# Three projections of a block by seven products, with the vector sums that they need, and a silu moved ahead

## The chip, the cores and the metric

The kernel runs on one core of one Trainium2 chip. The time is the device time of an execution in microseconds (us); the kernel before has a median of 972.35 us in three runs (972.24 to 972.92). The five engines of the core are named as the profile names them: PE (TensorE, with PEld for its weight loads), DVE (VectorE), ACT (ScalarE), POOL (GpSimd) and SP (SyncE, which issues the loads of weights).

## The reference, cut to what matters

Two blocks are computed one after the other on 256 tokens of width 1024, all in float32, each with two layers. The change lies in the first block:

```python
u = jnp.einsum('bsd,de->bse', h, w_in[l])
u_mla, u_sb, u_moba, u_conv, u_gate = jnp.split(u, SPLITS, axis=-1)
...
o_a = merge_heads(mla_attention(q_nope, q_rope, k_nope, k_rope, v_a))
...
o_b = merge_heads(stick_breaking_attention(split_heads(qb, H), split_heads(kb, H), split_heads(vb, H)))
...
qc, kc, vc = jnp.split(u_moba, 3, axis=-1)
o_c = merge_heads(moba_attention(split_heads(qc, H), split_heads(kc, H), split_heads(vc, H), rel_bias))
o_d = conformer_conv(u_conv, conv_dw_w[l], conv_dw_b[l], conv_ln_g[l], conv_ln_b[l],
                     conv_pw_w[l], conv_pw_b[l])
y = jnp.concatenate([o_a, o_b, o_c, o_d], axis=-1) * jax.nn.silu(u_gate)
y = jnp.einsum('bse,ed->bsd', y, w_out[l])
x = x + rms_norm(y, post_norm_g[l])
```

`h` is the normed input. Each of the four branches has four heads of 64, so a branch's queries, keys, values or gate are 256 columns of `u`. `conformer_conv` is a depthwise convolution of 31 taps over the tokens, a layer norm, a silu and a pointwise product. The second block needs products of a silu-ed row `c` with large matrices (`c_act @ w_ada`), whose results scale and shift its inputs.

## The kernel before, in words

**Units.** Weights come in units of 1 MB (128 partitions x 2048 floats) into a ring of six slots (`raw`). SP issues them strictly in order: unit n goes into slot n mod 6 once unit n - 6 is told as used (`used`). `ORDER` (L45) lists the 30 units of a layer of the first block: `w` is a unit of projection weights for PE, `a` a unit of the matrix for `c`, a column unit, which DVE multiplies by the row (`column_unit`, L977, two halves of 1024 by the custom instruction of L983). So column units fill DVE's free time in the first block.

**A projection** of 256 columns (`unit_t`, L1988) is sixteen PE products: for two halves of the columns and eight pieces of 128 inputs, the stationary side is 128x128 of weights, the moving side all 256 tokens of `hT`. It fills one bank of PSUM. Each float32 product shows as two records.

**A layer of the first block on PE**: transposes and the first projections, then queries and keys of the stick-breaking branch and its scores, then the third branch's queries and keys (U_CQ, U_CK) into banks G[0] and G[1], transposes of the first branch's queries and keys (L2173), the suffix sums of logarithms (L2179 to L2183), scores of heads 0 and 1 (`pair_scores`), and then four turns g = 0 to 3. A turn is one gate unit (L1996, 256 columns of `u_gate`, into G[1]), the products with values of the heads before (`pair_values`), the transposes of the probabilities of heads 2g and 2g + 1 (`turn`, L2023), in turn 0 the transposes of the convolution, in turn 2 those of its normed form, and the scores of heads 2g + 2 and 2g + 3. Before each gate unit but the first PE waits for `silu_ready`, value g: bank G[1] is free again. After the turns come the pointwise product (L2274), which waits for the silu on ACT, and the output product.

**DVE** in the same stretch: taps of the convolution (`taps`, L1025), rotary parts, column units, the sums around the logarithms (L1232, L1233, L1239), the three additions of L1245, and then a loop over the eight heads (from L1279): in even j the gate of turn j / 2 (`gate`, L1257, which tells `silu_ready`), maxima of heads j + 2 and j + 3 (`scores_max`, L1047 and L1050) and the inverses of their sums (L1057), a column unit; in j = 1 the statistics of the layer norm of the convolution (L1306), in j = 3 its normed form.

**ACT** copies banks, takes the exponentials, scales probabilities (`head_scaled`, L643 and L644), and computes a tanh of each gate unit (L780). After the last turn it computes the silu of the convolution (L800), with a load of its own table in front.

**Seven products.** The second block already computes its products of 2x2 blocks in a scheme of Strassen's kind: with both sides cut in two by two, seven products of sums of blocks take the place of eight. The sums of weights, of tokens and of results run on DVE. L1582 to L1588, L1750 to L1755 and L1763 to L1773 are such sums in the profile.

## Time and profile before

| | before |
|---|---|
| median of three runs | 972.35 us |
| the profiled execution | 971.84 us, its span 970.1 us |
| PE busy | 956.0 us, 99% |
| DVE busy | 759.1 us, 78% |
| ACT busy | 230.5 us, 24% |
| granted clock of PE, mean | 0.997 |

The span runs from the first to the last instruction; the execution's own time is 1.7 us longer. Times in the rows are us from the start of the span. A row of the timeline gives the start, the duration, engine, line, operation, what is written and read, and in brackets the idle time of that engine just before, with what ended it. A row with xN stands for N instructions that follow each other. The records of PE overlap at their ends, so the spacing of starts tells its pace, not the sum of durations.

### The profile page before, as it was taken

What the parts mean: (1) busy time and instruction counts of PE and PEld (TensorE: products, weight loads), DVE (VectorE), ACT (ScalarE), POOL (GpSimd) and SP (SyncE); (2) the same over time, 40 slices, a digit from 0 to 9 for tenths busy, and PEclk for the clock granted to TensorE, in tenths of its full rate; (3) what the DMA queues carried; (4) which work ended last, traced back from release to release, by engine and by line L of the source; (5) the groups of instructions that cost most, each with busy time, mean ns of one, the idle gap of its engine ahead of it and who ended that gap; (6) DMA issues with size and microseconds to landing.
All of it is one profiled execution on the core that took longest, in us unless ns stands there. A gap on an engine that the chain in (4) does not pass through costs nothing. (4 is left out here: it accounts for less than half of the span.)

```text
span 970.1 us, 14408 instructions
## 1 busy us (share of the span) xinstructions
PE 956.0 (99%) x5386; PEld 711.7 (73%) x5386; DVE 759.1 (78%) x1721; ACT 230.5 (24%) x580; POOL 83.0 (9%) x100
## 2 busy tenths in 40 slices
PE   8999999999999999999999999999999999999996
PEld 5858856858857998757777677689995767777764
DVE  2796687697688898999899988954667877766687
ACT  4134434125433222111000000124333200000002
POOL 2100000100001000000001000056830000000000
PEclk9999999999999999999999999999999999999998
DMA  9955553955555756473579776535443254644411
GB/s 354 379 197 201 221 213 133 370 200 227 195 215 208 296 219 258 175 301 132 217 289 362 293 271 252 203 131 195 153 174 131 100 204 174 217 174 174 174 44 44
DMA packets 31212, 205.38 MB, mean 212 GB/s; under 512 B 3655, under 2 KB 4860, under 8 KB 7852
## 3 DMA queue, kind: packets, MB, share of 16 engines
q1 hardware_dynamic: 27884, 190.94, 52.4%
q0 software_dynamic: 3264, 13.57, 3.8%
q8 instruction: 43, 0.70, 0.3%
q14 instruction: 21, 0.17, 0.0%
HBM read 203.42 MB, written 1.07 MB: 211 GB/s over the span
## 5 line engine op out<-in xcount | busy, mean ns | idle before, releaser
L1996 PE MATMUL bank<-hT,raw 128*128 128x256 f32 x704 | 155.6, 380 | 0.0
L1996 PEld LDWEIGHTS bank<-hT,raw 128*128 128x128 f32 x704 | 132.7, 190 | 20.1 <-issue 2.4
L983 DVE CUSTOM_DVE_ANT_0 raw<-raw,crow 128x1024 f32<-128x1024 f32 x96 | 113.8, 1229 | 10.5 <-DMA raw<-units_dram 9.1
L2355 PE MATMUL bank<-yT,arena 128*128 128x512 f32 x224 | 100.9, 593 | 0.7 <-DVE yT L1651 0.5
L2355 PE MATMUL bank<-raw,arena 128*128 128x512 f32 x180 | 86.8, 593 | 0.0
L2355 PEld LDWEIGHTS bank<-yT,arena 128*128 128x128 f32 x224 | 42.2, 190 | 54.0 <-issue 50.9
L2383 PEld LDWEIGHTS bank<-hT,raw 128*128 128x128 f32 x416 | 50.4, 192 | 11.5 <-issue 11.5
L840 ACT ACTIVATE arena<-bank 128x512 f32<-128x512 f32 x26 | 15.5, 598 | 178.5 <-PE bank L2383 178.5
L2383 PE MATMUL bank<-hT,raw 128*128 128x128 f32 x416 | 50.6, 275 | 0.0
L1025 DVE SCALAR_TENSOR_TENSOR arena<-arena 128x256 f32<-128x256 f32 x120 | 49.2, 486 | 0.1
L2355 PEld LDWEIGHTS bank<-raw,arena 128*128 128x128 f32 x180 | 30.1, 191 | 17.2 <-issue 17.2
L2383 PE MATMUL bank<-arena 128*128 128x128 f32 x336 | 42.1, 275 | 0.0
L2383 PE MATMUL bank<-arena,gateT 128*128 128x128 f32 x336 | 42.1, 275 | 0.0
L2383 PEld LDWEIGHTS bank<-arena 128*128 128x128 f32 x336 | 39.8, 192 | 1.2 <-issue 1.2
L2383 PEld LDWEIGHTS bank<-arena,gateT 128*128 128x128 f32 x336 | 39.8, 192 | 0.0
L2076 PE MATMUL bank<-arena 128*128 128x512 f32 x88 | 39.7, 592 | 0.0
L2383 PEld LDWEIGHTS bank<-arena,raw 128*128 128x128 f32 x224 | 29.4, 191 | 13.4 <-issue 13.4
L842 ACT ACTIVATE arena<-bank 128x384 f32<-128x384 f32 x28 | 13.8, 491 | 105.1 <-PE bank L2383 105.1
L2326 PE MATMUL bank<-hT,raw 128*128 128x128 f32 x244 | 37.4, 282 | 0.9 <-ACT hT L700 0.7
L1614 DVE TENSOR_TENSOR arena<-arena 128x256 f32<-128x256 f32 x26 | 11.0, 424 | 32.7 <-ACT arena L840 32.5
L2326 PEld LDWEIGHTS bank<-hT,raw 128*128 128x128 f32 x244 | 33.0, 191 | 3.8 <-issue 2.2
L2076 PEld LDWEIGHTS bank<-arena 128*128 128x128 f32 x88 | 16.6, 190 | 19.8 <-issue 19.7
(473 smaller groups left out, 1782.3 us busy)
## 6 DMA issues: line engine op xcount, KB each, us to landing
raw<-units_dram SPq DMA_DIRECT2D x178, 1024.0 KB, 4.9
arena<-ln_rows_dram POOLq DMA_DIRECT2D x4, 1024.0 KB, 5.7
arena<-gate_scratch POOLq DMA_DIRECT2D x4, 512.0 KB, 6.0
arena<-att_line_dram POOLq DMA_DIRECT2D x4, 512.0 KB, 5.9
arena<-small_dram POOLq DMA_DIRECT2D x2, 896.0 KB, 10.9
raw<-units_dram SPq DMA_DIRECT2D x2, 704.0 KB, 7.7
xt<-x_dram SPq DMA_DIRECT2D x2, 512.0 KB, 5.5
arena<-post_g_dram POOLq DMA_DIRECT2D x2, 512.0 KB, 8.7
```

Of the source, the lines that this page charges most:

```text
L840: act.activation(prod[:, 0:4].rearrange("p i n -> p (i n)"), A[0][:], ACT.Copy).then_inc(prod_ready.sem, 1)
L842: act.activation(prod[:, 4:7].rearrange("p i n -> p (i n)"), A[0][:, 0:3 * P], ACT.Copy).then_inc(prod_ready.sem, 1)
L983: ins = dve.tensor_tensor_reduce(out=w, in0=w, in1=crow[:], scale=1.0, scalar=0.0, op0=ALU.mult, op1=ALU.add, accum_out=dst[:, c:c + 1])
L1025: ins = dve.scalar_tensor_tensor(cacc[:, c, :], xg[:, c, j:j + S], w, cacc[:, c, :], ALU.mult, ALU.add)
L1614: ch.do(dve.tensor_tensor(csum[:, 0:5:4], p[:, 0:1].to_broadcast([P, 2, P]), p[:, 1:3], ALU.add))
L1996: mm = pe.matmul(b[:, c * S:(c + 1) * S], raw[:, s, k * 256 + c * P:k * 256 + (c + 1) * P], act_t[:, k, :], start=(k == 0), stop=(k == KC ...
L2076: mm = pe.matmul(OUT_BANKS[l][j][:], x[c] if isinstance(x, list) else x[:, c], y[c] if isinstance(y, list) else y[:, 512 * c:512 * (c + 1) ...
L2326: mm = pe.matmul(b[:, c * S + t * P:c * S + (t + 1) * P], raw[:, n % SLOTS, k * 256 + c * P:k * 256 + (c + 1) * P], hT[:, k, t * P:(t + 1) ...
L2355: mm = pe.matmul(SB[i][:], x, y, start=g == 0, stop=stop)
L2383: mm = pe.matmul(b[:, i * P:(i + 1) * P], x(k), y(k), start=k == 0, stop=k == 3)
```

## The change

**Units.** The order of the 30 units is new, with the same 18 and 12 of each kind, and three projection units are named for the new form: the third branch's queries and keys, and the second gate.

```diff
-ORDER = "wwwawwawwawawawa" "wawawawa" "wwawwa"
+ORDER = "wwwawwawwa" "wwwa" "wwaaa" "waa" "wa" "wwawwa"
...
+U_SEVEN = (U_CQ, U_CK, U_G1)
```

**DVE.** `first_tokens` makes four sums of `hT` once a layer, behind the rotary part of the keys. `first_weights` makes three sums from a unit of weights, and one in its place in the slot, as four instructions that each wait for the one before. `first_outputs` makes the four blocks of a result from seven products. Column unit 3 moves from between the taps to behind the first `first_outputs`, 4, 5 and 6 from around the logarithms to one place in j = 0 of the loop over the heads, 8 to j = 3. The last five taps move behind the sums of the logarithms. The second gate moves in j = 2 behind the maxima and inverses of heads 4 and 5.

```diff
+            def first_tokens(l):
+
+                dve.wait_ge(ht_act.sem, ht_act.at(l, 12))
+                dve.wait_ge(ht_dve.sem, ht_dve.at(l, 4))
+                b = [[hT[:, 4 * k:4 * k + 4, t * P:(t + 1) * P] for t in range(NT)] for k in range(2)]
+                ch.do(dve.tensor_tensor(first_tsum[:, 0], b[0][1], b[0][0], ALU.subtract))
+                ch.do(dve.tensor_tensor(first_tsum[:, 2], b[1][1], b[0][1], ALU.subtract))
+                ch.sync(1)
+                ch.do(dve.tensor_tensor(first_tsum[:, 1], b[1][1], first_tsum[:, 0], ALU.subtract))
+                ch.sync()
+                dve.tensor_tensor(first_tsum[:, 3], b[1][0], first_tsum[:, 1], ALU.subtract).then_inc(fsum_ready.sem, 1)
+
+            def first_weights(l, i):
+
+                wait_landed(dve, T1 * l, U_SEVEN[i])
+                ch.pass_waits()
+                a, d = first_blocks(U_SEVEN[i]), first_sums[i]
+                ch.do(dve.tensor_tensor(d[1], a[0][0], a[1][0], ALU.subtract))
+                ch.sync()
+                ch.do(dve.tensor_tensor(a[1][0], a[1][0], a[1][1], ALU.add))
+                ch.sync()
+                ch.do(dve.tensor_tensor(d[0], a[1][0], a[0][0], ALU.subtract))
+                ch.sync()
+                dve.tensor_tensor(d[2], a[0][1], d[0], ALU.subtract).then_inc(fsum_ready.sem, 1)
+
...
+
+                p, c = first_prod[i % 2], first_tmp
+                dve.wait_ge(fprod_ready.sem, fprod_ready.at(l, 2 * i + 2))
+                ch.pass_waits()
+                ch.do(dve.tensor_tensor(c[:, 0], p[:, 0], p[:, 2], ALU.add))
+                ch.do(dve.tensor_tensor(o[:, 0], p[:, 0], p[:, 1], ALU.add))
+                ch.sync(1)
+                ch.do(dve.tensor_tensor(c[:, 1], c[:, 0], p[:, 3], ALU.add))
+                ch.do(dve.tensor_tensor(c[:, 2], c[:, 0], p[:, 5], ALU.add))
+                ch.sync(1)
+                ch.do(dve.tensor_tensor(o[:, 2:4], c[:, 1:2].to_broadcast([P, 2, P]), p[:, 4:6], ALU.add))
+                ch.sync(1)
+                ch.do(dve.tensor_tensor(o[:, 1], c[:, 2], p[:, 6], ALU.add))
+                ch.sync()
+                dve.sem_inc(qk_ready.sem, 1)
+
...
-                taps(0, 12)
-                ada_unit(l, 3)
-                taps(12, 20)
+                taps(0, 20)
...
-                taps(20, TAPS)
-                ada_unit(l, 4)
+                first_weights(l, 0)
+                first_weights(l, 1)
+                taps(20, LATE_TAP)
...
-                ada_unit(l, 5)
-                ada_unit(l, 6)
+                taps(LATE_TAP, TAPS)
+                first_outputs(l, 0, qkC[:, 0].rearrange("p c (t n) -> p (c t) n", t=NT))
+                ada_unit(l, 3)
...
+                first_outputs(l, 1, qkC[:, 1].rearrange("p c (t n) -> p (c t) n", t=NT))
...
+                first_weights(l, 2)
                 for j in range(2 * H):
                     if j % 2 == 0:
-                        gate(j // 2)
+                        if j == 2:
+                            first_outputs(l, 2, early)
+                        else:
+                            gate(j // 2)
...
                             scores_max(j + 3)
                             head_inverse(8 * l, j + 2)
                             head_inverse(8 * l, j + 3)
+                        if j == 2:
+                            gate(1)
                         if j < 6:
-                            ada_unit(l, 7 + j // 2)
+                            for a in ((4, 5, 6), (7,), (9,))[j // 2]:
+                                ada_unit(l, a)
...
+                        ada_unit(l, 8)
```

**PE.** `first_seven` computes one unit as 28 products of 128 columns in two banks, in the place of sixteen of 256.

```diff
+            def first_seven(l, i, b0, b1):
+
+                u = U_SEVEN[i]
+                a, d = first_blocks(u), first_sums[i]
+                h = [[hT[:, 4 * k:4 * k + 4, t * P:(t + 1) * P] for t in range(NT)] for k in range(2)]
+                x = [first_tsum[:, k] for k in range(4)]
+
+                def product(b, c, w, y):
+                    for k in range(4):
+                        mm = pe.matmul(b[:, c * P:(c + 1) * P], w[:, k], y[:, k], start=k == 0, stop=k == 3)
+                    return mm
+
+                def first_bank():
+                    product(b0, 0, a[0][0], h[0][0])
+                    product(b0, 1, a[0][1], h[1][0])
+                    pe.wait_ge(fsum_ready.sem, fsum_ready.at(l, i + 2))
+                    product(b0, 3, d[1], x[2])
+                    return product(b0, 2, d[0], x[1])
+
+                def second_bank():
+                    product(b1, 0, a[1][1], x[3])
+                    pe.wait_ge(fsum_ready.sem, fsum_ready.at(l, i + 2))
+                    product(b1, 2, d[2], h[1][1])
+                    return product(b1, 1, a[1][0], x[0])
+
+                wait_landed(pe, T1 * l, u)
+                pe.wait_ge(fsum_ready.sem, fsum_ready.at(l, 1))
+                if i < 2:
+                    first_bank().then_inc(fhalf_ready.sem, 1)
+                    if i == 1:
+                        pe.wait_ge(fprod_ready.sem, fprod_ready.at(l, 2))
+                    second_bank().then_inc(used[u % SLOTS], 1)
+                else:
+                    second_bank().then_inc(fhalf_ready.sem, 1)
+                    if i > 2:
+                        pe.wait_ge(fprod_ready.sem, fprod_ready.at(l, 2 * i))
+                    first_bank().then_inc(used[u % SLOTS], 1)
+
...
+                first_seven(l, 0, G[0], G[1])
+                pe.wait_ge(upc_ready.sem, upc_ready.at(l, 6))
+                first_seven(l, 1, A[2], G[1])
...
-                    if g >= 1:
+                    if g == 0:
+                        pe.wait_ge(fprod_ready.sem, fprod_ready.at(l, 4))
+                    else:
                         pe.wait_ge(silu_ready.sem, silu_ready.at(l, g))
-                    unit_t(T1 * l, U_GATE[g], hT, G[1])
+                    if g == 1:
+                        pe.wait_ge(pt_ready.sem, 8 * l + 2 * g)
+                        first_seven(l, g + 1, G[1], A[0])
+                    else:
+                        unit_t(T1 * l, U_GATE[g], hT, G[1])
```

**ACT.** It copies the seven products out of the banks, computes the second gate's tanh from `gate_in` (the tile `early`, in SBUF) behind the copies of the probabilities, and the silu of the convolution in turn 2, ahead of the last tanh.

```diff
+                act.wait_ge(rope_ready.sem, rope_ready.at(l, 2))
+                for i, (u, b) in enumerate(((U_CQ, G[0]), (U_CK, A[2]))):
+                    scale = (HD_SCALE, 1.0)[i]
+                    act.wait_ge(fhalf_ready.sem, fhalf_ready.at(l, i + 1))
+                    act.activation(first_prod[i][:, 0:4].rearrange("p i n -> p (i n)"), b[:], ACT.Copy,
+                                   scale=scale).then_inc(fprod_ready.sem, 1)
+                    wait_used(act, T1 * l, u)
+                    act.activation(first_prod[i][:, 4:7].rearrange("p i n -> p (i n)"), G[1][:, 0:3 * P], ACT.Copy,
+                                   scale=scale).then_inc(fprod_ready.sem, 1)
...
+                def gate_copies(g):
+
+                    p = first_prod[(g + 1) % 2]
+                    act.wait_ge(qk_ready.sem, qk_ready.at(l, 2 + g))
+                    act.wait_ge(fhalf_ready.sem, fhalf_ready.at(l, g + 2))
+                    act.activation(p[:, 4:7].rearrange("p i n -> p (i n)"), A[0][:, 0:3 * P], ACT.Copy).then_inc(fprod_ready.sem, 1)
+                    wait_used(act, T1 * l, U_GATE[g])
+                    act.activation(p[:, 0:4].rearrange("p i n -> p (i n)"), G[1][:], ACT.Copy).then_inc(fprod_ready.sem, 1)
+
                 def gate_tanhs(g):
-                    wait_used(act, T1 * l, U_GATE[g])
+                    if g != 1:
+                        wait_used(act, T1 * l, U_GATE[g])
                     if g >= 1:
                         act.wait_ge(silu_ready.sem, silu_ready.at(l, g))
-                    act.activation(th[:].rearrange("p c s -> p (c s)"), G[1][:], ACT.Tanh, scale=0.5).then_inc(gate_tanh.sem, 1)
+                    if g == 1:
+                        act.wait_ge(qk_ready.sem, qk_ready.at(l, 5))
+                    act.activation(th[:].rearrange("p c s -> p (c s)"), gate_in if g == 1 else G[1][:], ACT.Tanh,
+                                   scale=0.5).then_inc(gate_tanh.sem, 1)
 
...
-                    gate_tanhs(g)
+                    if g == 1:
+                        gate_copies(g)
+                    else:
+                        gate_tanhs(g)
                     for j in (2 * g, 2 * g + 1):
                         head_copy(8 * l, j, (A[3], A[0]))
+                    if g == 1:
+                        gate_tanhs(g)
...
+                    if g == H - 2:
+                        act.preload_act_table_set("silu_and_others")
+                        act.wait_ge(cvp_ready.sem, cvp_ready.at(l, 2))
+                        for c in range(2):
+                            act.activation(zT[:, c, :], G[2][:, c * S:(c + 1) * S], ACT.Silu,
+                                           scale=col[:, C_LNG + c:C_LNG + c + 1],
+                                           bias=col[:, C_LNB + c:C_LNB + c + 1]).then_inc(z_conv.sem, 1)
```

**The rest.** Some semaphores are shared between events, so that the first copies into `hT` also wait for the load of `rel_bias`. In the second block one column unit is split over two groups.

```diff
+            ch.sync()
+            pool.dma_start(relb[0:NB, :], rel_bias).then_inc(pre_in, 16)
...
-            act.wait_ge(pre_in, 16 * DEPTH)
+            act.wait_ge(pre_in, 16 * (DEPTH + 1))
...
+                    if g in (7, 8):
+                        side_unit(lay, 7, (g - 7,))
+                    if g >= 8:
                         side_unit(lay, g)
```

How instructions moved: DVE of layer 0, kernel before, from the statistics of the convolution (j = 1) to the scores of heads 4 and 5 (j = 2). `probs` and `nm` are the scores and their maxima, `gateT` the gates.

```order
L1310 BN_AGGR bag<-bst 128x2 [waits dve_step]
L1312 TENSOR_SCALAR ms<-bag 128x2 [waits dve_step]
L1257 SCALAR_TENSOR_TENSOR gateT<-arena,bank 128x512 [waits gate_tanh]
L1047 ISA probs,nm<-bank,arena 128x128 [waits score_ready,ptp_ready]
L1050 ISA probs,nm<-bank,arena 128x256
L1057 RECIPROCAL rinv<-rsum 128x2 [waits exp_ready] x2
```

DVE of layer 0, the changed kernel, from the end of j = 0 to the second gate. The rows of L1023 are halves of column units, those of L1107 to L1115 are `first_outputs` into `early`.

```order
L1144 RECIPROCAL rinv<-rsum 128x2 [waits exp_ready] x2
L1023 ISA raw,acc<-raw,crow 128x1024 [waits landed4]
L1023 ISA raw,acc<-raw,crow 128x1024 [waits landed5]
L1023 ISA raw,acc<-raw,crow 128x1024 [waits landed0]
L1402 BN_STATS bst<-bank 128x6 [waits cvp_ready]
L1107 TENSOR_TENSOR arena<-arena 128x128 [waits fprod_ready]
L1115 TENSOR_TENSOR early<-arena 128x128 [waits dve_step]
L1134 ISA probs,nm<-bank,arena 128x128 [waits dve_step,score_ready,ptp_ready]
L1137 ISA probs,nm<-bank,arena 128x256
L1144 RECIPROCAL rinv<-rsum 128x2 [waits exp_ready] x2
L1346 SCALAR_TENSOR_TENSOR gateT<-arena,early 128x512 [waits gate_tanh]
```

Before, the second gate stood ahead of the maxima and inverses of heads 4 and 5, and one column unit stood between the first gate and it. Now it stands behind them, and three column units and the sums of the results stand between.

PE of layer 0, kernel before, from the transposes of heads 2 and 3 to the third gate unit:

```order
L2023 MATMUL bank<-kst,probs 128x128 [waits pt_ready,pn_ready]
L2023 MATMUL bank<-kst,probs 128x128 x2
L2197 MATMUL bank<-arena 128x128 [waits nm_ready]
L2199 MATMUL bank<-arena 128x256 x2
L1996 MATMUL bank<-hT,raw 128x256 [waits landed2,silu_ready]
L1996 MATMUL bank<-hT,raw 128x256 x15
```

The same place in the changed kernel:

```order
L2124 MATMUL bank<-kst,probs 128x128 [waits pt_ready,pn_ready,fprod_ready]
L2124 MATMUL bank<-kst,probs 128x128 x2
L2338 MATMUL bank<-arena 128x128 [waits qk_ready,nm_ready]
L2340 MATMUL bank<-arena 128x256 x2
L2097 MATMUL bank<-hT,raw 128x256 [waits landed1,silu_ready]
L2097 MATMUL bank<-hT,raw 128x256 x15
```

The order is the same: the scores of heads 4 and 5 (L2338, L2340), then the third gate unit, which waits for `silu_ready` with value 2, told by the second gate. The scores now also wait for the assembled queries and keys (`qk_ready`).

## Rows read from the trace of the kernel before

**Rows 1.** Waits of PE: who waited for whom, us in total, times, longest

```profile
PE bank L2274 <- ACT arena L800: 1.1, 2, 0.5
...
PE bank L2355 <- DVE yT L1651: 0.5, 1, 0.5
```

**Rows 2.** Timeline of PE, layer 0, second gate unit and what stands around it

```profile
96.44 0.82 PE L2023 MATMUL bank<-kst,probs 128*128 128x128 f32 x6
...
98.85 7.07 PE L1996 MATMUL bank<-hT,raw 128*128 128x256 f32 x32
105.84 0.65 PE L2205 MATMUL bank<-probsT,arena 128*64 128x256 f32 x4
...
109.61 7.17 PE L1996 MATMUL bank<-hT,raw 128*128 128x256 f32 x32
```

**Rows 3.** Timeline of PE, layer 1, a unit's products of 128 columns

```profile
161.92 3.73 PE L2061 MATMUL bank<-hT,raw 128*128 128x128 f32 x32
165.49 1.04 PE L2037 MATMUL bank<-kst,xs 128*128 128x128 f32 x8
```

**Rows 4.** Timeline of DVE, second block, sums of the seven-product scheme

```profile
321.47 0.69 DVE L1753 TENSOR_TENSOR gateT<-gateT,raw 128x512 f32<-128x512 f32 x1
322.19 0.69 DVE L1755 TENSOR_TENSOR gateT<-raw,gateT 128x512 f32<-128x512 f32 x1
...
332.07 0.29 DVE L1765 TENSOR_TENSOR arena<-arena,bank 128x128 f32<-128x128 f32 x1
...
333.83 0.69 DVE L1750 TENSOR_TENSOR arena<-raw 128x512 f32<-128x512 f32 x1 [0.22 <-DVE arena L1773]
```

**Rows 5.** Timeline of DVE, layer 0, from the last taps to the maxima of heads 4, 5

```profile
64.05 8.92 DVE L1025 SCALAR_TENSOR_TENSOR arena<-arena 128x256 f32<-128x256 f32 x22
...
75.18 0.69 DVE L1232 SCALAR_TENSOR_TENSOR arena<-bank,arena 128x512 f32<-128x512 f32 x1
75.78 0.69 DVE L1233 SCALAR_TENSOR_TENSOR arena<-bank,arena 128x512 f32<-128x512 f32 x1
...
80.30 1.22 DVE L983 CUSTOM_DVE_ANT_0 raw<-raw,crow 128x1024 f32<-128x1024 f32 x1
...
89.22 0.29 DVE L1047 CUSTOM_DVE_ANT_0 probs<-bank,kst 128x128 f32<-128x128 f32 x1
...
94.24 0.16 DVE L1057 RECIPROCAL rinv<-rsum 128x2 f32<-128x2 f32 x1
...
98.57 0.29 DVE L1047 CUSTOM_DVE_ANT_0 probs<-bank,kst 128x128 f32<-128x128 f32 x1 [0.55 <-PE bank L2015]
...
101.30 1.23 DVE L983 CUSTOM_DVE_ANT_0 raw<-raw,crow 128x1024 f32<-128x1024 f32 x1
...
103.60 0.76 DVE L1306 BATCH_NORM_STATS2 bst<-bank 128x6 f32<-128x256 f32 x2
...
109.89 0.29 DVE L1047 CUSTOM_DVE_ANT_0 probs<-bank,arena 128x128 f32<-128x128 f32 x1 [2.62 <-PE bank L2199]
```

**Rows 6.** Timeline of ACT, layer 0: the logarithm, the last scaled row of heads 0, 1

```profile
73.23 1.49 ACT L762 ACTIVATE arena<-arena 128x1536 f32<-128x1536 f32 x1
...
94.74 0.49 ACT L644 ACTIVATE probs<-probs,rinv 128x256 f32<-128x256 f32 x1
```

**Rows 7.** Stretches at the end (busy us by engine, PEclk, DMA), and PE's first weight loads

```profile
961.00:962.00 1.00, 0.79 (x2) 0.00 (x0) 0.89 (x5) 0.00 (x0) 0.00 (x0) 1.00 0.00 0
...
965.00:966.00 1.00, 0.00 (x0) 0.00 (x0) 0.93 (x5) 0.00 (x0) 0.00 (x0) 0.50 0.66 248
...
1.74 0.15 PEld L2029 LDWEIGHTS bank<-zeros 128*128 128x128 bf16 x1 [0.27 <-issue]
...
5.58 0.99 PEld L2029 LDWEIGHTS bank<-zeros 128*128 128x128 bf16 x5 [0.28 <-issue]
```

**Rows 8.** DMA issues: operation, times, KB each, us to landing

```profile
relb<-rel_bias_dram POOLq DMA_DIRECT2D x1, 0.5 KB, 6.1
...
raw<-units_dram SPq DMA_DIRECT2D x178, 1024.0 KB, 4.9
```

106 lines of the change are left out of this document (57 added, 49 removed).

## The prediction

> **What bounds the kernel now.** I read the waits of TensorE first. They come to a few us in the whole span, and two of the rows belong to places that the change touches: 1.1 us in two waits before L2274 (the pointwise product of the conformer branch, which waits for the silu of L800) and 0.5 us before one L2355 [rows 1]. TensorE is bound by its own work nearly everywhere, so its time falls only if its work or those waits fall, and every new wait on it is paid in full. I then read the timeline of TensorE and of VectorE side by side in the attention stage of layer 0, between 64 and 113 us [rows 2, 5]. The reader is to see two things. TensorE goes from one gate unit to the next with no idle time, and VectorE, which frees its banks, has only small gaps there. In layer 1 the same rows follow at the same distances, so I work out layer 0 and take it twice. 0.2% (2 us) is about what a measurement can tell from no change.
>
> **The work of TensorE.** The second gate unit takes 6.99 us as sixteen products of 256 columns, from 98.85 to 105.84 [rows 2]. The new form has 28 products of 128 columns, two records each. 32 such records take 3.57 us [rows 3], 0.1116 us each, so 56 take 6.25 us. That saves 0.74 us a unit, 2.2 us a layer (three units), 4.4 us in all. The silu, now ahead of the last tanh, takes away the 1.1 us at L2274: ScalarE does it while TensorE works on the last gate unit. The column unit split over two groups takes one half (1.15 us, below) out of the group before the 0.5 us wait at L2355, which is then gone. If all else were covered, the gain would be 4.4 + 1.1 + 0.5 = 6.0 us.
>
> **The work of VectorE, priced.** A sum of 128x512 that waits for the one before it takes 0.72 us (321.47 to 322.19) [rows 4], one that waits for nothing 0.60 (75.18 to 75.78) [rows 5]. One `first_weights` is 3 x 0.72 + 0.60 = 2.8 us. `first_outputs` is the row of sums from 332.07 to 333.83, 1.75 us [rows 4]. A column unit takes 2.3 us (101.30 to 103.60), and 2.5 with the gate column behind the fourth. One tap of one half takes 0.405 us (8.92 us for 22) [rows 5]. `first_tokens` is four sums, under 2.9 us, and lies far ahead of anything that waits. In all that is about 16.5 us more a layer on VectorE, so where it falls decides.
>
> **Up to the attention.** Before the logarithms VectorE loses column units 3 and 4 (4.8 us) and five taps (4.05 us), and gains two `first_weights` (5.6 us). It gets there at 75.18 - 4.8 - 4.05 + 5.6 = 71.9 and waits, since ScalarE's logarithm ends at 73.23 + 1.49 = 74.7 [rows 5, 6]. From there 5.1 us of sums (75.18 to 80.30) end at 79.9. Then come the five taps to 83.9, the first `first_outputs` to 85.7, unit 3 to 88.2 and the three additions of L1245 (0.6 us each) to 90.0, against 89.2 before. So exponential, head scores and scaling are 0.8 us late, while TensorE is 1.5 us early. It would come to the turn of the second head at 96.44 - 1.5 + 0.3 = 95.3, but the scaled rows end at 94.74 + 0.49 + 0.8 = 96.0 [rows 2, 6]. It waits 0.7 us and is ready for the second gate unit at 98.15. VectorE meanwhile ends the second inverse at 94.24 + 0.16 + 0.8 = 95.2, then does the third `first_weights` to 98.0 and the first gate to 98.6. TensorE starts the unit at 98.65, and of the 1.5 us gained 0.2 are left.
>
> **The place that decides.** TensorE's third gate unit still waits for `silu_ready` of the second gate. That gate on VectorE now stands behind the scores of heads 4 and 5 and their inverses. Those scores are the very products that TensorE issues just ahead of the third unit. So it must wait for a round trip through VectorE and ScalarE, which before it did not. TensorE: 98.65 + 6.25 + 3.77 (105.84 to 109.61) = 108.7 and it is there. VectorE: from the first gate at 98.6, maxima and inverses of heads 2 and 3 take 2.73 (98.57 to 101.30), to 101.35. Then it has three column units where it had one, 6.9, to 108.25. The statistics take 1.4 (0.76 and some short ones, estimated), to 109.6; the third `first_outputs` 1.75, to 111.35; maxima and inverses of heads 4 and 5 again 2.73, to 114.1; the second gate 0.65 (between the 0.60 and the 0.69 of such an instruction), to 114.75. TensorE starts at 114.8 instead of 109.61: idle for 6.1 us, and 5.2 us behind the kernel before, all gains so far counted in [rows 2, 5]. What waits behind it is everything: TensorE's queue is in order. With L2274's 0.54 us taken off, the layer costs 4.65 us. Two layers and the 0.5 us at L2355: 9.3 - 0.5 = **+8.8 us**.
>
> **The clock on top.** TensorE's last product ends at 961.8, and in the row from 965 the granted clock is 0.50, the 1.2 GHz level: about 3 us of idleness were enough [rows 7]. The idle 6.1 us are longer than that, so I expect the third gate unit to begin at 1.2 GHz. How long that lasts I take from the start of the kernel: the loads of weights for the warming products stand 0.43 us apart (0.15 and 0.28 idle) from the second at 1.74 on and close up only at 5.58. With the first, that is 4.2 us. Work at half rate for 4.2 us loses 2.1 us, **+4.2 us** for two layers. The bounds are 0 (clock kept) and twice that (the low stretch twice as long). The kernel shows no idle stretch of this length in its middle, and I take the start's value since it is the one measured climb. The Trainium skill, "TensorE: Matmul & The Clock Gate", "HAM oscillation — how this bites in real kernels", says that a wait that recurs sends TensorE back to half rate each time and each burst begins cold. By that rule the loss is paid twice. Without the rule, and with the clock kept, only the 8.8 us would stand.
>
> **What costs nothing.** The first copies into hT now also wait for the small load of `rel_bias`, which took 6.1 us to land [rows 8]. From its issue at 2.6 that is 8.7, which may delay them by half a us. I take 0, since TensorE's first tile is followed by a wait for its weights, and keep the half for the range. The new order of units is harmless: what VectorE or TensorE asks for in the stage was freed over 6 us earlier, and a unit lands 4.9 us after its issue [rows 8]. Units 4, 5 and 6 take the slots of V1 and of the third queries and keys, all done by 82. The last gate unit and the units of the output product shift with the rest. The silu moves with its own table load, so the count of loads stays. `first_tokens` of layer 0 fits where VectorE waits for the tanh of the conditioning row.
>
> **Sum.** Against the profiled execution's own 971.84 us: + 8.8 + 4.2 = 984.8. The median of the three runs lies 0.5 us above that execution, so I forecast **985.3 us**.
>
> **Rivals.**
> (1) The wait stands, but the clock holds in one or both idle stretches. For it: the fall came 3 us after the last product only at the one place where it can be read. Against: 6 us is twice that. Times: 972.35 + 8.8 + 2.1 = 983.3, or 981.2.
> (2) The wait is much shorter, because VectorE runs ahead of my sum (no wait at the logarithms, cheaper sums). The least it can be: scores are told at 109.89 - 2.2 = 107.7, then 2.73 and 0.65 give 111.1, 1.5 us behind before. With 0.54 off, twice, and 0.5 off: 972.35 + 1.4 = 973.8. An idle time of 3.7 us could still cost the clock. Against: the three column units alone take 6.9 us between the two gates.
> (3) Faster. The kernel ends on this side if the second gate were told before TensorE has issued the scores of heads 4 and 5. Then the 6.0 us stand and the time is 966.4. It decides from the point at which VectorE reaches that gate before 107.4 us. By the order of its instructions it can't, unless I misread which gate the third unit waits for. The rows before show the gate at no cost to TensorE, which is all that speaks for it.
> (4) Gains and wait cancel within 2 us: the least wait of (2) and some slack in the product sums that I priced at nothing, 972.
>
> **How the numbers follow.** My forecast has 0.60, rival (1) 0.20, (2) 0.10, (3) 0.06, (4) 0.04. The range takes in the forecast with a low stretch up to twice as long (989.5) or sums dearer by 0.2 us each, and rival (1) down to 981.2 with 1.5 us for my chain of VectorE: 979.5 to 990. That leaves out (2), (3) and (4), 0.2. Faster by over 0.2%: 0.06; within: 0.04; slower: 0.90.
>
> **What would show it.** In the profile after: idle time of some 6 us on TensorE before the first product of the third gate unit in each layer, put down to VectorE's gateT; a granted clock below 1.00 in the stretch behind it, with products of 256 columns at twice 0.22 us apart; 56 records of the second gate unit in 6.3 us; no wait at the pointwise product nor for yT L1651's counterpart. The forecast is wrong if TensorE has no wait of over 3 us there, and its clock part is wrong if the rows behind the wait stay at 1.00.

## The result, and the profile after

The changed kernel takes 984.9 us (median of 4 runs, 983.0 to 986.1), the kernel before 972.3 beside it. The ratio is 1.0126, with a 95% interval of 1.0114 to 1.0138: 12.6 us slower. The profiled execution of the changed kernel took 983.01 us, 11.2 above the profiled one before; it is the shortest of the four.

| | before | after |
|---|---|---|
| profiled execution, its span | 971.84, 970.1 us | 983.01, 981.2 us |
| third gate unit in layer 0 starts at | 109.61 | 115.03 |
| idle time of TensorE before it, in both layers | 0 | 11.3 us |
| the two waits of rows 1 | 1.1 and 0.5 us | 0 |

First the waits of TensorE in the changed kernel (waiting line, who released it, us in total, times, longest). L2097 is the product of a unit of 256 columns, L2124 the turn of a head; L2177, below, is `first_seven`.

```profile
PE bank L2097 <- DVE gateT L1346: 11.3, 2, 5.6
...
PE bank L2124 <- ACT probs L661: 0.7, 2, 0.4
```

A single place holds nearly everything, the third gate unit behind the gate of L1346. The waits for the silu and for yT, which stood in [rows 1], are gone.

The timeline of TensorE in layer 0, to be held against [rows 2]:

```profile
69.39 2.05 PE L2177 MATMUL bank<-hT,raw 128*128 128x128 f32 x16
...
82.00 1.93 PE L2314 MATMUL bank<-kst,arena 128*96 128x128 f32 x16
...
95.93 1.19 PE L2124 MATMUL bank<-kst,probs 128*128 128x128 f32 x6 [0.35 <-ACT probs L661]
...
99.11 1.16 PE L2177 MATMUL bank<-xs,raw 128*128 128x128 f32 x8 [0.24 <-DVE gateT L1346]
...
105.56 0.65 PE L2346 MATMUL bank<-probsT,arena 128*64 128x256 f32 x4
...
108.79 0.60 PE L2340 MATMUL bank<-arena 64*128 64x256 f32 x4
115.03 8.61 PE L2097 MATMUL bank<-hT,raw 128*128 128x256 f32 x32 [5.64 <-DVE gateT L1346]
123.57 0.65 PE L2346 MATMUL bank<-probsT,arena 128*64 128x256 f32 x4
...
162.18 1.09 PE L2138 MATMUL bank<-kst,xs 128*128 128x128 f32 x8
```

The third branch's two units last from 69.39 to 82.00, 12.61 us, where they took 13.92 (69.05 to 82.97). The second gate unit takes 6.45 us where it took 6.99. At 109.4 TensorE is done with the scores of heads 4 and 5 and stands until 115.03. From there thirty-two records take 8.54 us instead of 7.10. The next layer's first products start at 162.18, before at 155.90: +6.28, of which 0.34 stood already at the start of this stage (69.39 against 69.05). In layer 1 the same rows stand at 241.43 to 276.83, and the kernel is 12.55 us behind where that layer ends.

VectorE in the same stretch, to be held against [rows 5]:

```profile
75.09 0.69 DVE L1319 SCALAR_TENSOR_TENSOR arena<-bank,arena 128x512 f32<-128x512 f32 x1 [3.44 <-ACT arena L779]
...
98.37 0.68 DVE L1346 SCALAR_TENSOR_TENSOR gateT<-arena,bank 128x512 f32<-128x512 f32 x1
...
101.70 1.23 DVE L1023 CUSTOM_DVE_ANT_0 raw<-raw,crow 128x1024 f32<-128x1024 f32 x1
...
108.58 0.76 DVE L1402 BATCH_NORM_STATS2 bst<-bank 128x6 f32<-128x256 f32 x2
...
114.22 0.17 DVE L1144 RECIPROCAL rinv<-rsum 128x2 f32<-128x2 f32 x1 [0.71 <-ACT probs L654]
114.31 0.67 DVE L1346 SCALAR_TENSOR_TENSOR gateT<-arena,early 128x512 f32<-128x512 f32 x1
```

It idles 3.44 us before the logarithm sums, reaches the first gate at 98.37, does six halves of column units from 101.70 to 108.58, and comes to the second gate at 114.31, behind the last inverse of heads 4 and 5. The clock (stretch, its length, busy time of TensorE, weight loads, VectorE, ScalarE and GpSimd, granted clock, DMA share, GB/s):

```profile
114.00:115.00 1.00, 0.00 (x0) 0.00 (x0) 0.78 (x3) 1.00 (x5) 0.00 (x0) 0.78 1.02 426
115.00:116.00 1.00, 0.97 (x2) 0.83 (x3) 1.00 (x1) 0.57 (x2) 0.00 (x0) 0.50 1.03 434
...
118.00:119.00 1.00, 1.00 (x6) 0.87 (x6) 0.83 (x6) 0.00 (x0) 0.00 (x0) 1.00 0.00 0
...
264.00:265.00 1.00, 0.00 (x0) 0.00 (x0) 0.67 (x5) 0.60 (x1) 0.00 (x0) 0.87 1.02 434
...
268.00:269.00 1.00, 1.00 (x3) 0.82 (x4) 1.00 (x3) 0.49 (x2) 0.00 (x0) 0.50 1.06 451
...
271.00:272.00 1.00, 1.00 (x5) 0.77 (x5) 0.83 (x6) 0.00 (x0) 0.00 (x0) 0.71 0.00 0
```

TensorE's clock is at its lower level (0.50, 1.2 GHz) from 114.6 to 118.0 in layer 0 and from 264.7 to 271.6 in layer 1 (a row of 0.78 is the lower level for 0.44 of its us). It fell 5.2 us after the last product in the one and 2.4 us after it in the other.

### The profile page after: what moved, and what is told of

Read it like the earlier page. It is cut to its first block and busy times, and to the rows that moved or that the text cites. A ratio compares the mean times of both kernels' runs of the same rounds, so it can differ in the third digit from the quotient of the medians.

```text
span 981.2 us, 14852 instructions
## 1 busy us (share of the span) xinstructions
PE 955.7 (97%) x5530; PEld 715.9 (73%) x5530; DVE 786.5 (80%) x1789; ACT 234.1 (24%) x588; POOL 84.2 (9%) x100
## 3 DMA queue, kind: packets, MB, share of 16 engines
HBM read 203.42 MB, written 1.07 MB: 208 GB/s over the span
## 5 line engine op out<-in xcount | busy, mean ns | idle before, releaser
L2097 PE MATMUL bank<-hT,raw 128*128 128x256 f32 x512 | 116.5, 388 | 11.3 <-DVE gateT L1346 11.3
L1023 DVE CUSTOM_DVE_ANT_0 raw<-raw,crow 128x1024 f32<-128x1024 f32 x96 | 113.0, 1223 | 11.7 <-DMA raw<-units_dram 9.7
L2097 PEld LDWEIGHTS bank<-hT,raw 128*128 128x128 f32 x512 | 98.9, 195 | 27.1 <-DVE gateT L1346 12.1
L2532 PEld LDWEIGHTS bank<-hT,raw 128*128 128x128 f32 x416 | 50.4, 192 | 11.5 <-issue 11.5
L2475 PEld LDWEIGHTS bank<-hT,raw 128*128 128x128 f32 x244 | 33.0, 191 | 3.5 <-issue 2.1
```

What stands on the lines that cost most here:

```text
L1023: ins = dve.tensor_tensor_reduce(out=w, in0=w, in1=crow[:], scale=1.0, scalar=0.0, op0=ALU.mult, op1=ALU.add, accum_out=dst[:, c:c + 1])
L2097: mm = pe.matmul(b[:, c * S:(c + 1) * S], raw[:, s, k * 256 + c * P:k * 256 + (c + 1) * P], act_t[:, k, :], start=(k == 0), stop=(k == KC ...
L2475: mm = pe.matmul(b[:, c * S + t * P:c * S + (t + 1) * P], raw[:, n % SLOTS, k * 256 + c * P:k * 256 + (c + 1) * P], hT[:, k, t * P:(t + 1) ...
L2532: mm = pe.matmul(b[:, i * P:(i + 1) * P], x(k), y(k), start=k == 0, stop=k == 3)
```

## The experiments

Two questions were open. Does the idle stretch come from the order (a round trip through VectorE and ScalarE), or from VectorE's load? And is the clock a term of its own?

**1. The wait for the bank alone.** What the third gate unit really needs is its bank, and ScalarE has copied that long before.

```
+                    elif g == 2:
+                        pe.wait_ge(fprod_ready.sem, fprod_ready.at(l, 6))
                     else:
                         pe.wait_ge(silu_ready.sem, silu_ready.at(l, g))
```

> The changed kernel, but TensorE's third gate unit waits only until ScalarE has copied the bank G[1] of the second gate unit (fprod_ready), not for the second gate on VectorE. Theory (the round trip through VectorE sets the start): both idle stretches before this unit (5.6 us each in the profile of the changed kernel) go, and with them the low clock behind them (1.4 and 1.8 us there), so 984.9 - 11.3 - 3.2 = 970.4 us, the unit starts at once behind the scores at about 109.4 us, and takes 7.1 us. Rival (VectorE is simply too full): the idle time moves to the fourth gate unit or later, and the time stays above 980.

980.9 us, ratio 1.0087 (1.0070 to 1.0103); the text expected 970.4. TensorE, then VectorE, in that run:

```profile
109.05 7.17 PE L2097 MATMUL bank<-hT,raw 128*128 128x256 f32 x32
...
120.13 0.68 PE L2411 MATMUL bank<-kst,arena 128*128 128x128 f32 x4 [2.30 <-DVE arena L1412]
...
123.01 9.36 PE L2097 MATMUL bank<-hT,raw 128*128 128x256 f32 x32 [0.62 <-DVE gateT L1346]
```

```profile
114.03 0.67 DVE L1346 SCALAR_TENSOR_TENSOR gateT<-arena,early 128x512 f32<-128x512 f32 x1
...
119.08 1.00 DVE L1412 TENSOR_SCALAR arena<-bank,bag,rs 128x256 f32<-128x256 f32 x2
...
122.28 0.68 DVE L1346 SCALAR_TENSOR_TENSOR gateT<-arena,bank 128x512 f32<-128x512 f32 x1
```

The named wait went, in full: the unit starts at 109.05 and takes 7.10 us. But TensorE now stands at the transposes of `cnat` (the normed form of the convolution), 2.30 us, and then at the third gate, 0.62 (1.37 in layer 1), and the low clock is still there: the fourth gate unit takes 9.29 us. VectorE has column unit 7 between the second gate (114.03) and `cnat` (119.08). Of the 14.5 us expected, 4.0 came. The time is the one that the rival named (above 980), and the idle time did move on as it said. Neither theory stands alone: the wait was the order's, and behind it the load of VectorE was next.

**2. The second gate ahead of the maxima.**

```
                             first_outputs(l, 2, early)
+                            gate(1)
...
-                        if j == 2:
-                            gate(1)
```

> The changed kernel with VectorE's second gate directly behind the third first_outputs, ahead of the maxima and inverses of heads 4 and 5; TensorE's wait stays. Theory: the gate is told when ScalarE's tanh is done, about 112.8 instead of 114.9 us, so the idle stretch shrinks by 2.0 us to 3.6, in both layers: 984.9 - 4.0 = 980.9, and up to 3.2 less if the clock then holds. Rival (the bank or a DMA landing sets the start): no change, 984.9.

979.4 us, ratio 1.0071 (1.0055 to 1.0088). The idle stretch is 3.48 us, expected 3.6:

```profile
112.44 8.86 PE L2096 MATMUL bank<-hT,raw 128*128 128x256 f32 x32 [3.48 <-DVE gateT L1346]
```

The chain of VectorE is the one that sets the start. The clock was lost none the less: 8.79 us for the unit here and 10.2 in layer 1 (7.10 at full clock).

**3. Column units 5 and 6 behind the second gate.**

```
-                            for a in ((4, 5, 6), (7,), (9,))[j // 2]:
+                            for a in ((4,), (5, 6, 7), (9,))[j // 2]:
```

> The changed kernel with column units 5 and 6 of each layer moved behind the second gate (with unit 7), order and number kept. Theory (what stands on VectorE between the two gates sets the start): the gate is told 4.6 us earlier, at 110.3; the idle stretch is 1.0 us instead of 5.6, the clock stays at 1.00, and the time is 984.9 - 9.2 - 3.2 = 972.5. Rival (the order alone, a round trip that is long whatever stands between): most of the 5.6 us stays, over 978. Behind it 0 to 2 us could come back if the third gate, now behind three column units, is late.

981.0 us, ratio 1.0091 (1.0075 to 1.0108); expected 972.5, a miss. TensorE and VectorE:

```profile
112.13 8.86 PE L2097 MATMUL bank<-hT,raw 128*128 128x256 f32 x32 [3.59 <-DVE gateT L1346]
...
124.96 7.17 PE L2097 MATMUL bank<-hT,raw 128*128 128x256 f32 x32 [1.07 <-DVE gateT L1346]
```

```profile
105.56 0.29 DVE L1107 TENSOR_TENSOR arena<-arena 128x128 f32<-128x128 f32 x1 [1.06 <-ACT arena L805]
...
108.75 0.29 DVE L1134 CUSTOM_DVE_ANT_0 probs<-bank,arena 128x128 f32<-128x128 f32 x1 [1.76 <-DVEq L131]
...
111.41 0.67 DVE L1346 SCALAR_TENSOR_TENSOR gateT<-arena,early 128x512 f32<-128x512 f32 x1
```

VectorE is now early: it waits 1.06 us for the copies of the second gate unit and 1.76 us ahead of the first maximum, until TensorE's scores are there. The gate is told at 112.0 all the same, since maxima, exponentials and inverses of heads 4 and 5 follow on scores that TensorE issues at 107.6 to 108.5. So of 5.64 us of idle time, 3.6 are the round trip that the order makes, whatever VectorE's load, and 2.0 are the load. My 4.6 us had left out that the chain has a start on TensorE. And the third gate, now behind three column units, was 1.07 us late.

**4 and 5. The clock.** TensorE is kept busy in the idle stretch by products of zeros into the bank that is already copied, twelve of them in run 4 and 26 in run 5; the wait for the gate stays.

```
+                    elif g == 2:
+                        pe.wait_ge(fprod_ready.sem, fprod_ready.at(l, 6))
+                        for _ in range(12):
+                            pe.matmul(G[1][:], zeros[:, 0:P], zeros[:], start=True, stop=True)
+                        pe.wait_ge(silu_ready.sem, silu_ready.at(l, g))
```

> The changed kernel with twelve products of zeros (128 x 512 bf16) into the drained bank G[1] ahead of the same wait, so that TensorE works through the idle stretch (estimated 12 x 0.43 = 5.2 us of the 5.6) and then still waits for the second gate. Theory (an own term of the clock): the granted clock stays at 1.00, the third gate unit takes 7.1 us instead of 8.5 and 8.9, and the time is 984.9 - 3.2 to - 5 = 980 to 981.7. Rival (the unit is slow for another reason, such as memory traffic of the DMAs that land then): no change, 984.9 or a few tenths more.

982.5 us, ratio 1.0099 (1.0082 to 1.0115); expected 980 to 981.7, a miss. Twelve products took 2.76 us: I had taken 0.43 us for one, which is their distance at the start of the kernel, and at full clock it is half. So 2.94 us stayed idle, and the unit took 8.7 us, no less than in the changed kernel:

```profile
109.50 2.76 PE L2368 MATMUL bank<-zeros 128*128 128x512 bf16 x12
115.20 8.79 PE L2097 MATMUL bank<-hT,raw 128*128 128x256 f32 x32 [2.94 <-DVE gateT L1346]
```

> The run with twelve products of zeros again, with 26 of them: one took 0.22 us there (2.76 us for twelve), so 26 take 5.7 us and cover the idle stretch of 5.6. Theory (an own term of the clock): the granted clock stays at 1.00 and the third gate unit takes 7.1 us in both layers; the time is 984.9 - 3.2 to - 5 = 980 to 981.7. Rival (the unit is slowed by something else): it still takes over 8.5 us, 984.9.

979.8 us, ratio 1.0079 (1.0066 to 1.0092). With 26 of them TensorE has no idle stretch (the trace has records of 25 of them):

```profile
109.49 5.56 PE L2368 MATMUL bank<-zeros 128*128 128x512 bf16 x25 [0.16 <-issue]
114.98 7.17 PE L2097 MATMUL bank<-hT,raw 128*128 128x256 f32 x32
```

The clock in this run, and then a stretch of run 3 in its slow third gate unit:

```profile
115.00:116.00 1.00, 1.00 (x6) 0.90 (x6) 1.00 (x3) 0.52 (x2) 0.00 (x0) 1.00 1.03 434
```

```profile
113.00:114.00 1.00, 1.00 (x4) 0.82 (x3) 1.00 (x3) 0.00 (x0) 0.00 (x0) 0.50 0.00 0
```

The unit starts at the same time as in the changed kernel (114.98 against 115.03) and takes 7.10 us in both layers. The DMA share in the row from 115 is 1.03 in both kernels, at full clock here and at half there, and in run 3 the unit was slow with no transfer under way (0.00 from 113). So memory traffic isn't what slowed it. The clock's share of the change is the difference of the ratios, 0.0047 of 972.3 or 4.6 us (5.1 by the medians); the two intervals leave it uncertain by 1.7 us. In the profiled execution it is 1.4 + 1.8 = 3.2; that one had the highest mean clock of the four (0.993 against 0.991 and 0.992).

**6. Both bounds at once.** The wait of run 1, and

```
                 taps(20, LATE_TAP)
+                ada_unit(l, 3)
...
                 first_outputs(l, 0, qkC[:, 0].rearrange("p c (t n) -> p (c t) n", t=NT))
-                ada_unit(l, 3)
...
-                            for a in ((4, 5, 6), (7,), (9,))[j // 2]:
+                            for a in ((4, 5, 6), (7,), (8, 9))[j // 2]:
...
-                        ada_unit(l, 8)
```

> The changed kernel with three things moved: TensorE's third gate unit waits for the copied bank, as in the first experiment; column unit 3 goes ahead of the logarithm sums, where VectorE waits 3.4 us for ScalarE; column unit 8 goes behind the third gate. VectorE is then 2.3 us earlier at the scores of the first heads and another 2.3 us earlier at the third gate. Theory (two bounds, the wait on the gate and behind it VectorE's own work up to cnat and the third gate): both idle stretches of the first experiment (2.3 and 1.4 us) shrink under 0.5 us, the clock stays at 1.00, and the time is 972.35 - 6.0 + 0.3 (start of the kernel) = 966.7, up to 969. Rival (the stage is full on VectorE whatever the order): an idle stretch of over 2 us comes back at the inputs of the output product, and the time stays over 974.

972.4 us, ratio 1.0003 (0.9994 to 1.0011). 8.5 us better than run 1, and 5.7 short of the expectation. The rows of layer 0, then of layer 1:

```profile
118.51 0.98 PE L2410 MATMUL bank<-kst,arena 128*128 128x128 f32 x4 [2.28 <-DVE arena L1412]
...
121.01 7.70 PE L2096 MATMUL bank<-hT,raw 128*128 128x256 f32 x32
...
266.98 0.66 PE L2410 MATMUL bank<-kst,arena 128*128 128x128 f32 x4 [2.27 <-DVE arena L1412]
...
268.42 7.17 PE L2096 MATMUL bank<-hT,raw 128*128 128x256 f32 x32
```

`cnat` is still 2.3 us late, because I had moved unit 8 and not unit 7, which stands ahead of it. The two layers also show that the same wait may cost the clock or not: behind 2.28 us it took 10.13 us from the transposes to the end of the fourth gate unit (118.51 to 128.64), behind 2.27 it took 8.5, with the granted clock at 1.00:

```profile
118.00:119.00 1.00, 0.49 (x3) 0.49 (x4) 1.00 (x4) 0.00 (x0) 0.00 (x0) 0.85 1.10 459
119.00:120.00 1.00, 1.00 (x7) 0.67 (x7) 1.00 (x3) 0.00 (x0) 0.00 (x0) 0.50 0.98 410
...
268.00:269.00 1.00, 1.00 (x9) 0.62 (x6) 1.00 (x5) 0.00 (x0) 0.00 (x0) 1.00 1.06 451
```

**7. The silu alone**, in the kernel before: its table load and its two instructions behind the scaling of the last heads, ahead of the last tanh, as in the change.

> The kernel before with only the silu and its table load moved ahead of ScalarE's last tanh. Expected by the prediction's term: the two waits of 0.54 us before the pointwise product go and nothing else changes, 972.3 - 1.1 = 971.2. Rival (the tanh, now behind two loads and the silu, makes the fourth gate late): 972.3 or up to 1 us more.

971.35 us, ratio 0.9989 (0.9980 to 0.9998): 0.9 us faster where the term was 1.1. The wait for the silu is gone and the fourth gate unit starts 10.00 us behind the third, as before.

**8. The second gate unit by sixteen products again**, with its gate ahead of the maxima; queries and keys of the third branch stay in seven products.

```
-U_SEVEN = (U_CQ, U_CK, U_G1)
+U_SEVEN = (U_CQ, U_CK)
...
-                first_weights(l, 2)
...
-                        if j == 2:
-                            first_outputs(l, 2, early)
-                        else:
-                            gate(j // 2)
+                        gate(j // 2)
...
-                    if g == 1:
-                        pe.wait_ge(pt_ready.sem, 8 * l + 2 * g)
-                        first_seven(l, g + 1, G[1], A[0])
-                    else:
-                        unit_t(T1 * l, U_GATE[g], hT, G[1])
+                    unit_t(T1 * l, U_GATE[g], hT, G[1])
```

> The changed kernel with the second gate unit as sixteen products again, and its gate on VectorE ahead of the maxima as in the kernel before; the third branch's queries and keys stay in seven products. Theory: with the gate ahead of the scores the round trip is gone, and VectorE has 4.5 us less to do, so there is no idle stretch over 1 us and no low clock: 972.35 - 4 x 0.74 - 1.1 - 0.5 + 0.3 = 968.1, up to 970. Rival (the column units moved behind the logarithms alone make the wait): idle time of over 3 us stays before the third gate unit and the time is over 975.

971.8 us, ratio 0.9997 (0.9989 to 1.0006); expected 968.1. The long stall is gone with this one unit undone, though all column units stand where the change put them: they alone don't make it. (This run also takes 4.5 us of work from VectorE; that the rest was the gate's place is run 3's to show.) But four waits of 0.5 and 0.9 us stay, two in each layer; with the 0.36 at the turn of the second head, also in each, they come to 3.5 of the 3.7 us that are missing:

```profile
PE bank L2083 <- DVE gateT L1338: 2.8, 4, 0.9
```

**9. The same with column unit 3 ahead of the logarithm sums** (the first move of run 6).

> The changed kernel with the second gate unit as sixteen products, and besides column unit 3 ahead of the logarithm sums. VectorE is 2.3 us earlier from there on. Theory: the waits of 0.36, 0.51 and 0.91 us a layer of the run without this move go: 971.8 - 3.6 = 968.2. Rival (they are round trips between the engines that don't depend on VectorE's load): 971 to 971.8.

969.9 us, ratio 0.9975 (0.9966 to 0.9984), 1.9 us better than run 8, but through no gate: their waits are the same 2.8 us to the tenth. VectorE in that run:

```profile
96.61 0.69 DVE L1338 SCALAR_TENSOR_TENSOR gateT<-arena,bank 128x512 f32<-128x512 f32 x1 [2.93 <-ACT arena L811]
...
100.59 1.23 DVE L1015 CUSTOM_DVE_ANT_0 raw<-raw,crow 128x1024 f32<-128x1024 f32 x1
...
108.73 0.68 DVE L1338 SCALAR_TENSOR_TENSOR gateT<-arena,bank 128x512 f32<-128x512 f32 x1
```

The 2.3 us gained ahead are gone at 96.6, where VectorE waits 2.93 us for TensorE's first gate unit and then for its scores. From those scores on TensorE needs 10.8 us to the third gate unit (second unit, values, turns, scores), and VectorE 11.3 with its three column units (from 100.59), statistics and gate, whatever lead either had. The 1.9 us lie elsewhere: TensorE's wait at the turn of the second head (0.36 in each layer of run 8) is gone. From the first gate unit to the second TensorE takes 9.31 us in each layer (88.82 to 98.13), where run 8 took 10.20 (88.17 to 98.37). That is 1.8 us in all, more than twice the idle time that the wait shows.

**10. Unit 7 away from the path to `cnat`.** Run 6 with units 7 and 8 behind the scores of the last heads, and unit 9 beside unit 10, behind the weights of the output product.

```
-                            for a in ((4, 5, 6), (7,), (8, 9))[j // 2]:
+                            for a in ((4, 5, 6), (), (7, 8))[j // 2]:
...
+                ada_unit(l, 9)
                 ada_unit(l, 10)
```

> The kernel with three things moved, and of it column unit 7 moved from between the second gate and cnat to behind the scores of the last heads (with unit 8), and unit 9 to behind the weights of the second half of the output product. VectorE then has cnat ready 2.3 us earlier, at 116.1 us, when TensorE comes to its transposes (116.2), and the third gate at 116.7 against 117.6. Theory (work between two things that TensorE waits for, not the sum of VectorE's work): the two waits of 2.3 us at the transposes of cnat and the low clock behind them (about 1.3 us) go: 972.4 - 4.6 - 1.3 = 966.5. Rival (VectorE is full over the stage): the 2.3 us come back as waits for the inputs of the output product or at the end of the layer, and the time stays at 971 to 972.4.

970.0 us, ratio 0.9975 (0.9965 to 0.9985): 2.4 us of the 5.9 expected came. In the attention stage TensorE no longer stands: third and fourth gate units start 10.2 us apart (107.52 and 117.72). But the end of the layer shows the rest, xs (the scaled input) for the next layer 2.04 us late, and 6.2 us for products that take 4.8 at full clock:

```profile
155.37 1.38 PE L2138 MATMUL bank<-kst,xs 128*128 128x128 f32 x8 [2.04 <-DVE xs L1188]
156.58 6.39 PE L2150 MATMUL bank<-raw,hT 128*128 128x352 f32 x16
```

**11. The load of `rel_bias` with a semaphore of its own**, on top of run 10.

> The kernel with cnat's wait removed (unit 7 behind the scores of the last heads), and besides the load of rel_bias with a semaphore of its own again, so that the first copies into hT do not wait for it. Theory: TensorE's wait of 0.5 us for hT at its first tile goes back to 0.2 and the start is 0.3 us earlier: 966.5 - 0.3 = 966.2, which 5 rounds can hardly show, so the trace decides. Rival: the first tile waits for its weights anyway, no change.

970.2 us, ratio 0.9972 (0.9962 to 0.9981), no change against run 10. TensorE's wait for hT at its first tile was 0.54 us here and 0.17 in run 10, which had the shared semaphore. Among the other runs with the shared one it lies between 0.17 and 0.8. So the 0.5 us that the changed kernel shows there scatter from run to run and aren't shown to be the semaphore's.

**12. Unit 10 behind the first tile's normalization**, on top of run 10.

```
-                ada_unit(l, 10)
...
                     x_scale(l + 1, 0)
+                    ada_unit(l, 10)
```

and in the last layer behind `y_norm(l, 0)`.

> The kernel with unit 7 behind the scores of the last heads and unit 9 behind the weights of the output product, and besides column unit 10 moved from there to behind the first tile's normalization at the end of the layer, where VectorE had gaps of 0.6 and 1.5 us in layer 0 and 0.7, 0.4 and 1.1 in layer 1. Theory (VectorE's work may only stand where TensorE does not wait for it): the wait of 2.04 us for xs in layer 0, the low clock behind it (tile products of 6.39 us instead of 4.97, 1.4 us) and the wait of 0.8 us in layer 1 go: 970.0 - 4.2 = 965.8. Rival (the work only moves the wait to the second tile): waits of the same size stand at the second tile of each layer and the time stays at 969 to 970.

968.97 us, ratio 0.9963 (0.9949 to 0.9977): faster than the kernel before by 3.0 us and the best of this study. 1.0 us of the 4.2 expected came. The first tile now starts without a wait and at full clock, but behind it stand 0.89 us for hT and 0.43 for a load, and 0.70 us for hT in layer 1:

```profile
158.57 2.60 PE L2152 MATMUL bank<-raw,hT 128*128 128x352 f32 x8 [0.89 <-ACT hT L702]
161.61 3.84 PE L2164 MATMUL bank<-hT,raw 128*128 128x128 f32 x32 [0.43 <-DMA raw<-units_dram]
```

## Why the prediction was right

The forecast was 985.3 us, the kernel takes 984.9. The mechanism was the one named, and the terms came near. The timeline adds up as 2 x 4.5 for the layers, 3.2 for the clock, 0.34 at the start of the kernel, and less 0.8 for yT (its wait of 0.53 and slower records behind it) and some 0.55 that are won back in pieces of up to 0.3 us behind the second layer, which no wait explains: 11.2 us, the difference of the profiled executions.

That the number is right to 0.4 us is in part luck. The sum for the profiled execution was 984.8, and it took 983.01, 1.8 us less; but its median lies 1.9 us above that execution, where the text had allowed 0.5.

| step | prediction | measured |
|---|---|---|
| seven products, three units a layer | -2.2 a layer | -1.31 - 0.54 = -1.85 |
| silu (L2274) | -1.1 | -1.1 in the profile, -0.9 alone (run 7) |
| yT (L2355) | -0.5 | the wait is gone, -0.8 by the timeline |
| wait at the turn of head 1 | 0.7 | 0.35 told as idle, 0.5 by the timeline, and 0.37 for slower records behind it |
| second gate unit starts | 98.65 | 99.11 |
| TensorE reaches the third | 108.7 | 109.4 |
| second gate told, third unit starts | 114.75, 114.8 | 114.9, 115.03 |
| idle before it | 6.1 | 5.64, both layers |
| a layer without the clock | +4.65 | 6.28 - 0.34 - 1.44 = 4.5, in layer 1 12.55 - 6.28 - 1.78 = 4.5 |
| clock, both layers | +4.2 | 3.2 in the profile, 4.6 by run 5 |
| merged semaphore | 0 to 0.5, taken as 0 | no effect seen (run 11) |

**VectorE's sum held.** Three column units took 6.88 us against 6.9, statistics with the short ones 1.3 against 1.4, `first_weights` 2.77 against 2.8, `first_outputs` 1.76 against 1.75, and the gate came within 0.2 us. Prices read from rows of the same shape and the same kind of wait carry over.

**One piece of it was left out, and didn't show.** Ahead of the first maxima stands the second `first_outputs`, which the part "Up to the attention" doesn't count. So the maxima begin at 92.07, 2.85 us later than before (89.22), and not 0.8. VectorE, then ScalarE, in the changed kernel:

```profile
92.07 0.29 DVE L1134 CUSTOM_DVE_ANT_0 probs<-bank,kst 128x128 f32<-128x128 f32 x1 [0.33 <-DVEq L131]
```

```profile
91.94 1.28 ACT L817 ACT_TABLE_LOAD   x1
93.24 0.40 ACT L652 ACTIVATE probs<-probs,nm 128x128 f32<-128x128 f32 x1
```

ScalarE loads a table until 93.2 and takes the exponentials only then, so the missing 1.75 us were hidden there. The second inverse ends at 95.6 against 95.2 predicted, and 0.34 of that is the start of the kernel. That it cost nothing was luck.

**TensorE's gain was too large by a sixth.** The 0.1116 us a record are [rows 3]'s, from 32 records in a row. The 112 records of the first two units took 12.61 us against 12.50 at that pace, without any wait, and the 56 of the second gate unit 6.45 against 6.25: 0.1 us for its first eight (99.11 to 100.10) and 0.1 for its last. The small waits also moved the timeline by more than the idle time told: 0.35 us of idleness stood for 0.5 us of delay and 0.37 of slower records behind it, 0.24 for 0.4. TensorE was at the second gate unit 0.46 us later than predicted, of which 0.34 are the start of the kernel, and at the third 0.7. VectorE's gate was told only 0.15 later, so the idle stretch is shorter by 0.5. The end is set by VectorE, so none of this showed in the sum.

**The clock's term was right in kind and loose in size.** The text took one low stretch of 4.2 us from the start of the kernel. Layer 0 had 3.4 us and layer 1 6.8, of which TensorE worked in 3.0 and 3.6. The start's 4.2 us were themselves read from the distance of its products (0.43 us against 0.22 in run 4); the granted clock of those rows is 1.00 in the profile. The rule of "TensorE: Matmul & The Clock Gate", "HAM oscillation — how this bites in real kernels", in the Trainium skill, that each recurring wait is followed by a cold burst, agrees with both layers here (granted clock 0.50 in the rows from 115 and from 268). Run 6 bounds it: of two waits of 2.3 us one was followed by a low clock and one was not.

**The rivals.** That the clock holds (1) is refuted by the granted clock and by run 5. That VectorE runs ahead and only the round trip stays (2) is what run 3 made: the prediction had 3.7 us of idleness as its least, and 3.59 came. Its time of 973.8 had no clock in it, and run 3 took 981.0. The clock makes 4.2 of these 7.2 us in the profile. The rest is of the size of two small waits that the rival had at nothing (1.3 us a layer) and of the third gate that came late (1.07 and 0.28 us). The forecast of a shorter wait was right, its price was not. That the gate is told in time (3) was ruled out by the order, and run 1 shows that even a wait on the bank alone doesn't bring its 966.4: the next waits on VectorE took most of it.

## What to carry to other kernels

When a step is moved behind work that depends on what the waiting engine issues last, price the round trip first (3.6 us here): no lightening of the other engine takes it away. Then ask what the wait protects; where it is a bank, wait for the copy, not for the last user of the copied values. And go on down the other engine's list to the next thing the first one needs: taking away the first wait gave 4.0 us, taking away what stood ahead of the next ones another 12 (runs 6, 10 and 12).

An idle stretch of a few us on TensorE has two prices, its own length and the half-speed work behind it, and the second doesn't shrink with the first: 5.6 us of idleness cost 1.4 to 1.8 us of clock in the profiled run, 3.5 us cost 1.7 to 3.1, and 2.3 us (run 6) 1.6 or nothing.

## What was unexpected of the hardware

The clock's loss followed no simple function of the wait. Idle time, and what TensorE's work from there to the end of the next gate unit took beyond its time at full clock, in layers 0 and 1:

| run | idle | loss |
|---|---|---|
| changed kernel | 5.64, 5.64 | 1.4, 1.8 |
| 2 | 3.48, 3.50 | 1.7, 3.1 |
| 3 | 3.59, 3.59 | 1.7, 2.5 |
| 4 | 2.94, 2.95 | 1.6, 1.7 |
| 1 | 2.30 + 0.62, 2.30 + 1.37 | 3.0, 3.1 |
| 6 | 2.28, 2.27 | 1.6, 0 |

In the changed kernel the clock had fallen 0.5 us before TensorE resumed in layer 0 and 3.2 us before in layer 1, after idle stretches equal to 0.01 us. In layer 0 of run 6 it fell only 0.2 us after TensorE had resumed (0.85 in the row from 118 is the lower level for its last 0.3 us). Where it falls decides how much of the low time meets work; what sets that point stays open.

Whether it also makes the scatter of the executions isn't shown. For it: the twelve of run 6 lie between 970.0 us at a mean granted clock of 0.998 and 975.3 at 0.993, and the four of the changed kernel between 983.0 at 0.993 and 986.1 at 0.991. Against: runs 2 and 3 have stretches of 3.5 us and scatter by 0.7 and 1.1 us, no more than run 5 without one (1.2), and in run 3 the execution at 0.997 took 980.8 us, those at 0.992 980.6 and 981.2. With the 4.2 us of loss in the table it should have been faster by most of that. So the loss is shown in the profiled executions and, for the changed kernel, by run 5; how large it is in any other execution is not.
